# FFN of a hybrid S5/Hyena block on one core: activation loads on their own semaphores, x back in halves, four output banks, splits of h's sums between weight slices

## The reference, cut to what matters

```python
x = x + gate_mix[:, None] * mixer_output(u_x, y_x, hy_x, gates_x, lp)
x = x + gate_ffn[:, None] * swiglu(modulate(x, norm_ffn[l], shift_ffn, scale_ffn),
                                   w_ffn_in[l], w_ffn_out[l])
...
def swiglu(h, w_in, w_out):
    a, b = jnp.split(h @ w_in, 2, axis=-1)
    return (jax.nn.silu(a) * b) @ w_out
...
return rms_norm(x, norm_f)
```

## Time and profile before

| What | Value |
|---|---|
| Median of 3 runs | 2896.37 us (2891.21 to 2899.15) |
| The profiled execution's own time | 2897.78 us |
| Its span | 2896.0 us |
| PE busy in the span | 2821.0 us, 97% |
| DVE busy | 1939.7 us, 67% |
| ACT busy | 970.8 us, 34% |
| Mean granted clock of PE | 0.991 |
| Moved by DMA | 473.73 MB, mean 164 GB/s |

### The profile page before, as it was taken

The page is one execution under the profiler, slowest core; times in us unless marked ns, Lnnn a source line. Parts: engine busy times, 40 slices in busy tenths (PEclk is TensorE's granted clock), DMA queues, the critical chain, the costliest instruction groups (busy, mean ns, idle before and its releaser), DMA issues.

```text
span 2896.0 us, 40851 instructions
## 1 busy us (share of the span) xinstructions
PE 2821.0 (97%) x17044; PEld 2454.9 (85%) x17044; DVE 1939.7 (67%) x2657; ACT 970.8 (34%) x1376; POOL 272.3 (9%) x474
## 2 busy tenths in 40 slices
PE   7999999999999999999989999999999999999997
PEld 3688888888888888887879999999999987888886
DVE  6556676985443777887677888888887773333445
ACT  4332333224432522221153443434444342222221
POOL 0002331001233001111000000000000000000000
PEclk9999999999999999999999999999999999999998
DMA  9736974334446437886544444444443335434333
GB/s 408 288 101 150 194 180 133 122 122 129 133 146 199 169 125 275 298 281 244 196 152 149 139 143 148 144 142 140 149 135 117 117 115 187 134 98 138 95 98 111
DMA packets 139387, 473.73 MB, mean 164 GB/s; under 512 B 24401, under 2 KB 24657, under 8 KB 134594
## 3 DMA queue, kind: packets, MB, share of 16 engines
q1 hardware_dynamic: 84226, 302.96, 31.7%
q0 software_dynamic: 47104, 156.09, 16.6%
q10 hardware_dynamic: 7872, 12.06, 1.2%
HBM read 426.53 MB, written 44.43 MB: 163 GB/s over the span
## 4 chain that ended last, share of the span: by engine, by line
PE 88%; DVE 5%; DMA 4%; ACT 2%; issue 1%; POOL 0%; DVEq 0%; SPq 0%; ACTq 0%; POOLq 0%
PE ps L2040 11%; PE ps L2042 11%; PE ps L2041 11%; PE ps L2295 9%; PE ps L2297 9%; PE ps L2296 9%; PE ps L2325 5%; PE ps L2326 5%; PE ps L2327 5%; PE ps L2057 2%; DMA hw_raw<-in_w_in 1%; PE ps L2010 1%; PE ps L2119 1%; PE ps L2058 1%; PE ps L1951 1%
## 5 line engine op out<-in xcount | busy, mean ns | idle before, releaser
L1118 DVE TENSOR_TENSOR hw_lo<-hw_raw,hw_hi 128x1024 fp32r<-128x1024 f32 (+1 forms) x348 | 382.8, 1102 | 641.3 <-ACT hw_hi L678 639.2
L678 ACT ACTIVATE hw_hi<-hw_raw 128x1024 fp32r<-128x1024 f32 (+1 forms) x348 | 334.0, 962 | 1055.4 <-DMA hw_raw<-in_w_in 465.4
L1048 ACT ACTIVATE wx_hi<-wx 128x1024 fp32r<-128x1024 f32 x287 | 303.8, 1059 | 450.0 <-PE ps L2297 431.3
L1765 DVE TENSOR_TENSOR wx_lo<-wx,wx_hi 128x1024 fp32r<-128x1024 f32 x287 | 350.4, 1221 | 59.7 <-ACT wx_hi L1048 59.7
L2295 PE MATMUL ps<-t_hi,wx_hi 128*128 128x256 f32 x1312 | 371.3, 283 | 0.0
L2296 PE MATMUL ps<-t_lo,wx_hi 128*128 128x256 f32 x1312 | 371.3, 283 | 0.0
L2297 PE MATMUL ps<-t_hi,wx_lo 128*128 128x256 f32 x1312 | 371.3, 283 | 0.0
L2040 PE MATMUL ps<-h_hi,hw_hi 128*128 128x512 f32 x896 | 353.7, 395 | 3.2 <-DVE st_b L1383 1.9
L2042 PE MATMUL ps<-h_hi,hw_lo 128*128 128x512 f32 x896 | 350.3, 391 | 0.0
L2041 PE MATMUL ps<-h_lo,hw_hi 128*128 128x512 f32 x896 | 349.6, 390 | 0.0
L2325 PE MATMUL ps<-act_hi,hw_hi 128*128 128x512 f32 x704 | 275.8, 392 | 12.6 <-DVE hw_lo L1118 7.1
(11 more groups left out here) (359 smaller groups left out, 5182.3 us busy)
## 6 DMA issues: line engine op xcount, KB each, us to landing
wx<-in_w_fi SPq DMA_DIRECT2D x164, 512.0 KB, 3.3
hw_raw<-in_w_in SPq DMA_DIRECT2D x128, 512.0 KB, 4.2
ada1m<-in_w_ar POOLq DMA_DIRECT2D x128, 512.0 KB, 4.9
ada_mix<-in_w_ac SPq DMA_DIRECT2D x16, 2048.0 KB, 12.7
hw_raw<-in_w_fo SPq DMA_DIRECT2D x64, 384.0 KB, 3.1
hw_raw<-in_w_fo SPq DMA_DIRECT2D x64, 320.0 KB, 2.9
hw_raw<-in_w_glu SPq DMA_DIRECT2D x32, 512.0 KB, 4.7
hw_raw<-in_w_out SPq DMA_DIRECT2D x32, 512.0 KB, 4.4
```

Source lines behind the costliest of these rows:

```text
L678: act.activation(hw_hi[slot(n)][:, 0:width(n)], hw_raw[slot(n)][:, 0:width(n)], ACT.Copy).then_inc(w_hi, 1)
L1118: tt(hw_lo[s][:, 0:w], hw_raw[s][:, 0:w], hw_hi[s][:, 0:w].bitcast(F32), SUB).then_inc(w_lo, 1)
L1765: tt(wx_lo[o % 12][:, :], wx[o % 12][:, :], wx_hi[o % 4][:, :].bitcast(F32), SUB).then_inc(w_lo, 1)
```

## The change

Four edits, all in the FFN.

1. `h_sums_hi`: on ACT the four splits of h's sums are spread out between the splits of slices `N_HU+8` to `N_HU+11`.
2. `load_act`: each of the three loads of a quarter counts on a semaphore of its own, `act_in[c]`, and `act_hi(q, k)` waits for the load that brings tile k. In quarter 0 ACT and DVE split d0 after the eighth tile, no longer after the eleventh.
3. x comes back in two halves with a semaphore each, issued as soon as the last first-product operand is used (`w_used` at `N_D`), ahead of the last tile's store. `down` waits for the half that it needs.
4. The second product uses four PSUM banks, `ps[m % 4]`, and PE waits for the output four tiles back.

```diff
-    xs_out, xs_in = tf_in
-    act_in, act_st = x0_in, uh_in
+    xs_out, xs_in = tf_in[0], [tf_in[1], tg_in[1]]
+    act_in, act_st = [x0_in[0], x0_in[1], tg_in[0]], uh_in
...
-            for k in range(3):
-                pool.wait_ge(w_used, N_D - 6 + k)
-                load_act(0, 4 * k, min(4 * k + 4, QTILES))
+            for c in range(3):
+                pool.wait_ge(w_used, N_D - 6 + c)
+                load_act(0, c)
+            pool.wait_ge(w_used, N_D)
+            for half in range(2):
+                pool.dma_start(xout[:, 8 * half:8 * half + 8, :], xs_d[:, 8 * half:8 * half + 8, :]).then_inc(xs_in[half], 16)
             store_act(TILES - 1)
-            pool.wait_ge(w_used, N_D)
-            pool.dma_start(xout[:, :, :], xs_d).then_inc(xs_in, 16)
...
-                act.wait_ge(act_in[q % 2], 16 + 48 * (q // 2 + 1))
+                act.wait_ge(act_in[k // 4], 32 + 16 * q)
...
-            for c in range(4):
-                h_sums_hi(c)
+            h_sums_hi(0)
             split_hi(N_HU + 8)
+            h_sums_hi(1)
             split_hi(N_HU + 9)
+            h_sums_hi(2)
             ffn_silu(1)
             split_hi(N_HU + 10)
+            h_sums_hi(3)
             split_hi(N_HU + 11)
...
-            for k in range(QTILES):
+            for k in range(ST):
                 act_hi(0, k)
             split_hi(N_D)
+            for k in range(ST, QTILES):
+                act_hi(0, k)
             split_hi(N_D + 1)
...
-                elif m == 0:
-                    dve.wait_ge(xs_in, 32)
-                stt(xout[:, m, :], ps[m % 2][:, :], mod_x[:, 5 * KT + m:5 * KT + m + 1], xout[:, m, :],
+                elif m % 8 == 0:
+                    dve.wait_ge(xs_in[m // 8], 32)
+                stt(xout[:, m, :], ps[m % 4][:, :], mod_x[:, 5 * KT + m:5 * KT + m + 1], xout[:, m, :],
...
-                    n, out = N_D + 2 * KT * q + 2 * m, ps[m % 2][:, :]
-                    if KT * q + m >= 2:
-                        pe.wait_ge(fd_free, KT * q + m - 1)
+                    n, out = N_D + 2 * KT * q + 2 * m, ps[m % 4][:, :]
+                    if KT * q + m >= 4:
+                        pe.wait_ge(fd_free, KT * q + m - 3)
```

More of the change, by code:

```diff
@@ L299, in block_kernel @@
     uh_in, x0_in, tf_in, tg_in = ([sem(f"{n}{j}") for j in range(2)] for n in ("uh_loaded_or_act_stored", "x0_loaded_or_act_loaded",
-        "tf_loaded_or_xacc_moved", "tg_loaded"))
+        "tf_loaded_or_xacc_moved", "tg_loaded_or_act_or_xacc_loaded"))
     tb_hi, tb_lo = sem("table_hi_ready"), sem("table_lo_ready")
@@ L646, in store_act, with load_act @@
                 pool.dma_start(act_d[:, g, :], f_t[g % 2][:, :]).then_inc(act_st[g % 2], 16)
-            def load_act(q, k0, k1):
+            def load_act(q, c):
+                k0, k1 = 4 * c, min(4 * c + 4, QTILES)
                 pool.dma_start(a_raw[q % 2][k0 // ST][:, k0 % ST:k0 % ST + k1 - k0, :],
-                               act_d[:, QTILES * q + k0:QTILES * q + k1, :]).then_inc(act_in[q % 2], 16)
+                               act_d[:, QTILES * q + k0:QTILES * q + k1, :]).then_inc(act_in[c], 16)
             for g in range(TILES - 1):
@@ L669, in _ @@
                     pool.wait_ge(w_used, N_D + 2 * KT * (q - 1))
-                for k in range(3):
-                    load_act(q, 4 * k, min(4 * k + 4, QTILES))
+                for c in range(3):
+                    load_act(q, c)
         @block.scalar
@@ L1851, in _ @@
                         ada_row(N_WIDE + p)
-            for k in range(QTILES):
+            for k in range(ST):
                 act_lo(0, k)
             split_lo(N_D)
+            for k in range(ST, QTILES):
+                act_lo(0, k)
             split_lo(N_D + 1)
```

## The result

| | before | after |
|---|---|---|
| Median of 9 runs each, taken side by side | 2902.15 us (2891.21 to 2905.27) | 2881.9 us (2876.67 to 2891.63) |
| Ratio, 95% interval | | 0.9941 [0.9924, 0.9958] |
| The profiled execution's own time, span | 2897.78, 2896.0 us | 2887.76, 2886.0 us |
| From plain tile 1's first matmul to the last addition to `xout` | 1374.2 us | 1356.2 us |

The account below looks back on a forecast made before the run. PE was 88% of the chain, so only its waits and low clock could be won: 4.1 + 8.3 + 7.8 = 20.2 us off 2897.8 gives 2877.6, less 1.4 for the median, 2876.2 us; range 2868 to 2888.

Parts of the forecast that it names:

- if PE waits over 2 us at d2, d3 or d4: Second product: sign that the prediction is wrong, a PE wait over 2 us at one of these three weight slices.
- The other signs: FFN profile: no wait on tile 2's line, second product within 0.5 us of pairs, clock 1.00, x's halves before d4.
- Edit 1: First product, plain tile 2: PE's 2.5 us wait and 1.6 us of slow clock go, gain 4.1 us.
- Edit 2: Start of the second product: 6.9 us of wait and 1.7 of clock won, less 0.3, gain 8.3 us.
- d2, costed at 0.3 us: Second product: slice d2, the tightest, ready at 2385.7 against PE asking at 2385.6; 0.3 us put on it.
- Edits 3 and 4: Second product, 5.4 us wait put down to `xout`: that wait and 2.4 us of clock go, gain 7.8 us.
- d4 ... with the start-up (... about 1) at 2390: Second product: d4, issued at 2382.2, takes 8 turns of 0.85 us plus about 1 of start-up, landing at 2390.
- The banks at 0: Second product: four banks cost at 0, hidden by x's earlier landing; up to 5.4 us were x late by 5.
- Slices late behind x: Rival, second product: d3 and d4 wait for all of x; gain 13.1 us, time 2883; chance 0.11.
- The slower case: Rival, second product: each slice beside POOL's traffic takes 13.4 us; +7, 2904 us; chance 0.03.
- my own model: DMA queues beside x: two queues take turns one row at a time, some 0.85 us per 16 KB row of x.

Follow-up runs that it names:

- e1: The kernel before with only the high parts of h's sums spread between the splits of the last plain slices; ratio 0.9982, tile 1 to pairs 43.7 us.
- f2: The kernel before with only the activation loads on semaphores of their own and d0 split after the eighth tile; ratio 0.9976, down to add 487.8 us.
- f4: The kernel before with activation loads on their own semaphores and four PSUM banks, x whole and late; ratio 0.9967, down to add 484.9 us.
- e2: The changed kernel with two PSUM banks in the second product instead of four; ratio 0.9947, sum of stretches 1356.8 us.
- e3: The changed kernel with x in one 4 MB transfer with 32 KB rows, issued at the same early place; ratio 0.9960, down to add 483.6 us.
- g3: The changed kernel once more, unchanged, beside the same runs of the kernel before; ratio 0.9939, median 2880.6 us, down to add 481.8 us.
- f1: The changed kernel with x's second half issued behind quarter 1's loads, once d7 has been used; ratio 0.9925, down to add 479.2 us.
- g1: The changed kernel with both halves of x issued when d0 is used, as d4 is, not one slice earlier; ratio 0.9935, median 2877.93 us.
- e4: The changed kernel with x in eight transfers with 4 KB rows, issued at the same place; ratio 0.9930, down to add 479.2 us.
- g2: The changed kernel with x's second half behind quarter 1's loads and each half in four transfers with 4 KB rows; ratio 0.9932, median 2876.76 us.

## Why the prediction was right, and where its size was off

Forecast: 20.2 us of gain, 2876.2 us. Measured: 17.1 us (12.2 to 22.1) by the ratio and 18.0 us in the stretch. That the median of 2881.9 us lies 5.7 above the forecast is mostly the ground that it stood on: the kernel before took 2896.37 us as the median of the runs shown then, and 2902.15 beside the changed one. The ratio times 2896.37 is 2879.3.

The prediction's own list of what would show it did not hold at one place. It called itself wrong "if PE waits over 2 us at d2, d3 or d4", and PE waited 2.7 us for d4, which landed at 2397.4 and not before 2391. The other signs came: x's halves ahead of d4 (by 0.2 us), the first matmul of the second product, the clock at 1.00 between 2350 and 2450, ACT's splits in three groups, no wait at tile 2 or the pairs. So the time and edits 1 and 2 came out for the reasons given, and edits 3 and 4 won 2.6 us less than forecast.

- **Edit 1, 4.1 us (2.5 of wait, 1.6 of clock).** Right: 4.3 in the stretch of after and of e1. PE's low parts are in time, and the pairs start without a wait. The clock's part is less certain than I made it, since f2 to f4 had the wait without the fall.
- **Edit 2, 8.3 us.** The mechanism is right: ACT's splits come in groups by landing, and PE goes from the pairs to d0 in 0.35 us. The stretch up to there gave 7.1 against 6.9 forecast. The 1.7 us of clock behind it came too, since nothing stands at the start any more. d2, costed at 0.3 us, did not show: DVE did d2 and d3 from 2387.84 to 2389.5, so d2 was through at 2388.7, and PE asked for it at 2388.8. But the edit is not worth this by itself: f2 shows that without edit 3 the second product gives most of it back at tile 2.
- **Edits 3 and 4, 7.8 us.** This is the term that was mis-sized. From down to add the forecast was 9.2 us (5.4 + 2.4 + 1.7 - 0.3) and the trace shows 6.6. The step that failed was "d4 ... with the start-up (... about 1) at 2390": 7.8 us from issue to landing; it took 11.7. In after's own time, it was asked for at 2385.65 and due by 2394.7 if PE was not to wait; it landed at 2397.4. PE asked nearly when forecast: it was through with tiles 0 and 1 15.4 us behind the first matmul, forecast 14.9.
- **The banks at 0.** Right within 0.5 us (e2), and for the reason given: x lands in time. With x late they were worth 3 us (f4), where I had allowed up to 5.4.
- **The rivals.** "Slices late behind x" named the right thing at too high a price and one slice too many: d3, issued with x, landed in 2.9 us, and only d4 was late. The slower case is out: no slice took 13.4 us.

**Where d4's 3.9 us come from.** The queues in after, from 2384 to 2388, from 2388 to 2389, from 2389 to 2394, and then the line of all packets in 2395 to 2396 and in 2396 to 2397.4:

```profile
q0 software_dynamic: 104, 1.70, 100.3%
...
q0 software_dynamic: 39, 0.39, 92.5%
q8 instruction: 1, 0.02, 6.0%
...
q0 software_dynamic: 110, 1.79, 88.2%
q1 hardware_dynamic: 98, 0.30, 15.4%
...
DMA packets 154, 0.41 MB, mean 405 GB/s; under 512 B 20, under 2 KB 20, under 8 KB 153
...
DMA packets 161, 0.42 MB, mean 300 GB/s; under 512 B 28, under 2 KB 28, under 8 KB 160
```

First, no packet of q1 before 2389.2, 3.5 us after the issue, though the engines were at work for POOL all the time; the forecast had about 1. Then turns, 110 to 98 in 5 us, as the earlier trace rows had them. A turn took 5 x 16 / 110 = 0.73 us, where the forecast had 0.85, x's whole 14.0 us divided by its rows. By 2395.4 fifteen of the sixteen engines had set d4's end mark: 6.2 us for this part against 6.8. And last a remainder: one packet in each of the last two lines is not under 8 KB, a row of x, while all others are rows of slices or the end of the store. They belong to a single engine that is behind the others: it set d4's mark at 2397.4, 2.0 us after the fifteenth. Forecast 1 + 6.8, measured 3.5 + 6.2 + 2.0; the differences are 2.5 - 0.6 + 2.0 = 3.9.

The late engine has a neighbour in the traces: the line `q8 instruction: 1` above is a packet of 16 KB on the instruction queue, started at 2388.7, which held one engine for 0.96 us while half 0 of x was running. Every trace has one such packet near the start of the second product. Where it fell into x's large rows, the last engine brought d4 1.7 to 2.0 us after the fifteenth (after, e2, e3, g3), and 1.0 us in f1, where it came as x's last rows ended; where it came before x, the slice beside x was in on all engines within 0.3 us (before, e1, f2, f4, g1). With rows of 4 KB it cost 0.0 (e4) and 0.6 us (g2). That is what thirteen executions have in common and not an experiment: no run moved this packet by itself, and why 1 us of it should cost 2 stays open. If the link holds, some 2 of the 2.7 us that PE waited are not due to the meeting of x and d4 alone.

What is shown by intervention: that d4 is late where x stands ahead of it in the DMA engines (g1, which moves the same bytes by one slice: 3.1 us), that less x (f1) or smaller rows (e4) shorten it, and that larger rows don't lengthen it much (e3). How these runs divide between the first packet, the turns and the late engine is read from the traces alone. The first packet's delay goes by time more than by rows: 3.5 us with rows of 4 KB (e4), 3.5 with 16 KB (after; 3.4 for d5 in g1), 3.5 with 32 KB (e3). It is no constant either: 2.9 in before and 4.9 in e1, both with 32 KB, 2.8 in g2 with 4 KB, and 1.9 in f1, where x's rows ran out. With POOL's queue empty it was 0.95 to 0.97 us each time. What sets it stays open.

The Trainium skill, "DMA: Bandwidth & Descriptors", section on queues, rings and completion order, has an engine drain a packet of typically 9 to 17 descriptors from one ring before it turns to another. Turns of 110 to 98 in 5 us, while half 1 of x and d4 were both there, don't fit it, as the earlier trace rows did not. And under it the first row of a slice would be held up by the rest of x's packet: e4 moved 1.29 MB in 3.5 us, so that its transfers of 512 KB, eight rows of 4 KB for each engine, pass in 1.4 us, and yet the slice's first packet was not seen for 3.5 us. One thing does fit it: where the slice was first, in g1, each engine finished its part of d4 before its first row of x. So the rule doesn't explain the delay; my own model, which had turns from the start, doesn't either.

## What to carry to other kernels

Time a transfer that must be in soon by its neighbours, not by its size. Asked for 4 us behind x, a slice took 11.7 us; 0.3 us ahead of x, 3.1 (d4 in g1). By these runs the order counts and not the closeness: asked for 0.4 us behind x, with the last store just ahead of both, a slice took 13.5 to 13.8 us (before, f2, f4). If a bulk transfer isn't urgent, issue it behind the small one that is, or cut it, and count every slice that will be asked for while it runs. Where several waits follow each other, one edit alone may only push the time into the next (f2); cost them as a chain, and try each alone before you judge it.

## What the runs showed of the hardware that was not expected

- A slice asked for on SP's queue while POOL's transfers filled the DMA engines, or began to within 0.2 us, sent its first packet 2.8 to 4.9 us later in eleven traces, where a free queue gave it 0.95 to 0.97; it did not follow the row size (3.5 us with 4, 16 and 32 KB). In f1 it came after 1.9 us, when x's rows ran out.
- A slice asked for 0.3 us ahead of x was wholly in after 2.9 to 3.5 us (d3 in the eight traces with an early x other than g1; d4 in g1), and in g1 each engine began with x only when its part of the slice was through. Asked for 0.4 us behind x it took 13.5 to 13.8 us (before, f2, f4).
- A packet of 16 KB on the instruction queue, 0.96 us on one DMA engine, goes with one late engine: d4's last part came 1.7 to 2.0 us after the fifteenth in the four traces where that packet fell into x's rows of 16 or 32 KB. Not shown by an experiment.
- The clock is not a fixed price of a wait: behind 2.4 to 2.5 us ahead of tile 2 it fell in before and not in f2 to f4; at output tile 2 it did not fall behind 2.7 us in after, 2.8 + 0.5 in e2 and 2.3 + 0.4 in g3, behind 2.5 + 1.0 in e3 and 3.8 + 1.0 in f4 it did, for 3.4 us each, and behind 6.5 + 1.2 in f2 for 6.8.
- The part ahead of tile 1 varies by 10.5 us between executions (1498.0 to 1508.5), more than any single edit here is worth; the stretch from tile 1 to the last addition repeats within 0.1 us where the kernels agree (after and g3: 1356.2 and 1356.1), its parts within 0.4.
